# Layer 1's gate and up products as seven block products, with plain f32 products in seven gate tiles and in half of the mixer

## The reference, cut to what matters

```python
def swiglu(h, w_in, w_out):
    gu = h @ w_in                                   # (544, 1024) @ (1024, 5632)
    return (jax.nn.silu(gu[..., :D_FF]) * gu[..., D_FF:]) @ w_out

def pool_mixer(xn, hist, pos, c_w, c_scale):        # layer 1's mixer C
    ...
    y = jnp.einsum('btgc,gce->btge', d, c_w).reshape(b, t, D_MODEL) * c_scale
    return y, ext[:, -C_HIST:]

for layer in range(DEPTH):
    ...
    hp = hp + rms_norm(mp, g[1])
    hp = hp + rms_norm(swiglu(rms_norm(hp, g[2]), ffn_w_in[layer], ffn_w_out[layer]), g[3])
```

## Time and profile before

| | us |
|---|---|
| median of 3 runs | 990.38 (990.16 to 990.46) |
| the profiled execution's own time | 990.5 |
| its span in the trace | 988.6 |
| PE busy | 970.2 (98%) |
| DVE busy | 687.3 (70%) |
| ACT busy | 539.0 (55%) |

### The profile page before, as it was taken

One profiled execution on the slowest core, in us unless ns is written; L12 is line 12 of the kernel. 1 busy time (PEld: TensorE's weight loads), 2 busy tenths in 40 slices (PEclk: granted clock), 3 DMA queues, 4 the chain that ended last, 5 costly groups with the idle time before them and its releaser, 6 DMA issues.

```text
span 988.6 us, 18137 instructions
## 1 busy us (share of the span) xinstructions
PE 970.2 (98%) x7314; PEld 938.8 (95%) x7314; DVE 687.3 (70%) x1024; ACT 539.0 (55%) x979; POOL 49.2 (5%) x57
## 2 busy tenths in 40 slices
PE   7999999899999999999999999999999999999997
PEld 6799899899999999999999999999999999999886
DVE  5487554788799998876599877888755545444643
ACT  5632665666555555466567665775544444444542
POOL 0080220100000000000000000002000000000000
PEclk9999999999999999999999999999999999999999
DMA  8324122556544544357654685666565555556653
GB/s 271 85 69 112 44 65 65 157 166 174 156 128 142 141 134 133 106 164 201 177 167 143 173 213 161 177 174 192 165 175 169 167 160 148 147 165 186 202 171 133
DMA packets 268339, 150.21 MB, mean 152 GB/s; under 512 B 14874, under 2 KB 259458, under 8 KB 268256
## 3 DMA queue, kind: packets, MB, share of 16 engines
q1 hardware_dynamic: 267792, 148.60, 52.0%
q0 software_dynamic: 224, 0.35, 0.1%
q10 hardware_dynamic: 240, 0.10, 0.0%
HBM read 146.45 MB, written 2.58 MB: 151 GB/s over the span
## 4 chain that ended last, share of the span: by engine, by line
PE 92%; DVE 4%; ACT 2%; DMA 1%; issue 1%; ACTq 0%; DVEq 0%
PE ps L746 23%; PE ps L748 22%; PE ps L747 22%; PE ps L1227 6%; PE ps L1229 6%; PE ps L1228 6%; DVE wlo L1959 1%; PE ps L1181 1%; PE ps L1183 1%; PE ps L1182 1%; DMA raw<-in_ffn_w_in_dram 1%; ACT whi L1378 1%; PE ps L996 1%; DMA scale_rows<-in_c_scale_dram 1%; PE ps L940 1%
## 5 line engine op out<-in xcount | busy, mean ns | idle before, releaser
L1959 DVE TENSOR_TENSOR wlo<-raw,whi 128x1024 fp32r<-128x1024 f32 (+3 forms) x278 | 300.4, 1083 | 164.0 <-ACT whi L1378 163.6
L1378 ACT ACTIVATE whi<-raw 128x1024 fp32r<-128x1024 f32 (+3 forms) x278 | 257.5, 930 | 142.2 <-PE ps L748 120.0
L746 PE MATMUL ps<-xhi,whi 128*128 128x256 f32 (+2 forms) x968 | 282.4, 292 | 0.5 <-DVE wlo L1959 0.5
L748 PE MATMUL ps<-xhi,wlo 128*128 128x256 f32 (+2 forms) x968 | 278.2, 287 | 0.0
L747 PE MATMUL ps<-xlo,whi 128*128 128x256 f32 (+2 forms) x896 | 257.6, 287 | 0.0
L746 PEld LDWEIGHTS ps<-xhi,whi 128*128 128x128 f32 x968 | 182.1, 188 | 2.8 <-issue 0.9
L748 PEld LDWEIGHTS ps<-xhi,wlo 128*128 128x128 f32 x968 | 182.0, 188 | 0.0
L747 PEld LDWEIGHTS ps<-xlo,whi 128*128 128x128 f32 x896 | 168.6, 188 | 0.0
L747 PE MATMUL ps<-mlo,whi 128*128 128x256 f32 (+1 forms) x352 | 101.0, 287 | 0.0
L746 PE MATMUL ps<-mhi,whi 128*128 128x288 f32 (+1 forms) x280 | 81.9, 292 | 0.0
L748 PE MATMUL ps<-mhi,wlo 128*128 128x288 f32 (+1 forms) x280 | 81.5, 291 | 0.0
(11 more groups left out here) (294 smaller groups left out, 1981.1 us busy)
## 6 DMA issues: line engine op xcount, KB each, us to landing
raw<-in_ffn_w_in_dram SPq DMA_DIRECT2D x110, 512.0 KB, 4.0
raw<-in_ffn_w_in_dram SPq DMA_DIRECT2D x88, 256.0 KB, 3.4
raw<-in_ffn_w_out_dram SPq DMA_DIRECT2D x48, 384.0 KB, 3.6
raw<-in_ffn_w_out_dram SPq DMA_DIRECT2D x48, 320.0 KB, 3.2
raw<-in_ffn_w_out_dram SPq DMA_DIRECT2D x22, 512.0 KB, 4.4
raw<-in_ab_w_in_dram SPq DMA_DIRECT2D x10, 512.0 KB, 4.8
raw<-in_ab_w_out_dram SPq DMA_DIRECT2D x10, 256.0 KB, 2.9
raw<-in_ab_w_out_dram SPq DMA_DIRECT2D x20, 128.0 KB, 3.3
```

What stands on the lines that cost most here:

```text
L746: pe.matmul(out, wh, xh, start=first, stop=False)
L748: return pe.matmul(out, wl, xh, start=False, stop=last)
L1378: act.activation(whi[:, m % NSPLIT, 0:n], split_source(m), ACT.Copy).then_inc(w_hi, 1)
L1959: dve.tensor_tensor(wlo[:, s, 0:n], split_source(m), whi[:, s, 0:n].bitcast(F32), ALU.subtract)\
```

## The change

Layer 1's gate and up go the way of layer 0's: `fast_first(1)` and `fast_rest(1)` stand where the two passes stood. Half 1's norms and mixer, which had the 44 slots of pass (1,0), have 22 now: STAGE[1,1] is compressed into slots 1 to 16, STAGE[2,1] has its sum at 16 and its residual additions up to slot 21, and everything from `fold` on stands at slots 22 and later, that is, behind the loop over the gate tiles. `splits(1)`, high and low parts of the inner activations, go with `ffn_out(1,1)`.

Units named in PLAIN are not split: PE multiplies the raw f32 tile by the raw f32 x (`xa[1]`), one instruction per chunk in place of three (the trace counts a plain f32 product as two records). Such a tile's place is free only when PE has used it. Mixer C's product for half 1 is plain too, from the raw x (`xf`), its weights from a tile of its own (`c_tile`) and from raw place 3, loaded on ACT's queue.

```diff
-FAST = (0,)
-EARLY = 13
+FAST = (0, 1)
+PLAIN = (5, 7, 9, 12, 15, 17, 19)
...
-    (1, 1): {"sum": 2, "spread": 4, "scale": (4, 5, 7, 8), "fold": 10, "pre": 12, "again": 14, "x": (14, 15, 16, 17),
-             "hist": 9, "rows": (10, 11), "keep": (15, 16),
-             "windows": (20, 23, 24), "ends": (21, 25), "post": (23, 24, 25, 26), "add": (24, 25, 26, 27)},
-    (2, 1): {"sum": 29, "spread": 31, "scale": (31, 32, 34, 35), "fold": 37, "pre": 39, "again": 41,
-             "x": (41, 42, 43, 44)},
+    (1, 1): {"sum": 1, "spread": 3, "scale": (3, 4, 5, 6), "fold": 7, "pre": 7, "again": 9, "x": (9, 9, 10, 11),
+             "hist": 4, "rows": (8, 9), "keep": (9, 10), "c": (11, 12),
+             "windows": (12, 13, 14), "ends": (13, 14), "post": (13, 14, 14, 15), "add": (14, 15, 15, 16)},
+    (2, 1): {"sum": 16, "spread": 18, "scale": (18, 19, 20, 21), "fold": 22, "pre": 22, "again": 23,
+             "x": (23, 24, 25, 26), "s1": (27, 28), "s2": (29, 30), "s34": (31, 32)},
...
+SPLIT_UNITS = [unit[0] != "p" or unit[1] == 0 or unit[2] not in PLAIN for unit in UNITS]
...
-            n = min(range(NRAW if r in FOUR_TILES else NRAW - 1), key=lambda n: (max(last[2 * n:2 * n + 2]), n))
+            n = key[1] % (NRAW - 1) if kind == "p" else \
+                min(range(NRAW if r in FOUR_TILES else NRAW - 1), key=lambda n: (max(last[2 * n:2 * n + 2]), n))
...
-                        sp.wait_ge(w_lo, AT[("tc" if kind == "u2" else kind, *key)] + 1)
+                        m = AT[("tc" if kind == "u2" else kind, *key)]
+                        if SPLIT_UNITS[m]:
+                            sp.wait_ge(w_lo, split_no(m))
+                        else:
+                            sp.wait_ge(w_used, m + 1)
...
+            def plain_pool_products(j):
...
+                        mm = pe.matmul(flat(ring[e % len(ring)], 0, n), tile[:, w], xf[:, 2 * g + k, CUT:CUT + n],
+                                       start=k == 0, stop=k == 1)
...
+                        if plain:
+                            mm = pe.matmul(out, raw_part(load_of(m), UNIT)[:, w], xa[layer][:, k, 0:CUT],
+                                           start=opens and k == ks[0], stop=closes and k == ks[-1], skip_group_check=True)
+                            continue
...
-            ffn_in(1, 0, stepper(pooling(1)))
-            ffn_in(1, 1, idle)
-            ffn_out(1, 1, idle)
+            fast_first(1, stepper(pooling(1)))
+            fast_rest(1)
+            ffn_out(1, 1, stepper(splits(1)))
```

More of the change, by code:

```diff
@@ L122, in unit_sequence @@
     for layer in range(2):
[L123 to L132, removed]
+        seq += [("p", layer, f) for f in range(FC)]
+        for f in range(FC):
+            seq += [("ta", layer, f)] + [("tc", layer, f - 1)] * (f > 0) + [("tb", layer, f)]
+        seq.append(("tc", layer, FC - 1))
         for b in FO_ORDER[layer]:
@@ L166, in split_count @@
 def split_count(layer, b, f):
[L168 to L172, removed]
-    return before + (f + 1 if f < EARLY else EARLY + (f - EARLY) // 2 + 1)
-SPLITS = EARLY + len(LATE) + len(PAIRS)
+    before, early = SPLITS[0] * layer, EARLY[layer]
+    if b != layer:
+        return before + early + len(LATE[layer]) + f // 2 + 1
+    return before + (f + 1 if f < early else early + (f - early) // 2 + 1)
+SPLITS = [early + len(late) + len(PAIRS) for early, late in zip(EARLY, LATE)]
 def z_count(s, d):
@@ L232, in load_of @@
     return LOAD_AT[("u2", *unit[1:]) if unit[0] == "tc" else unit]
[L235 removed]
+FOUR_TILES = [r for r, load in enumerate(LOADS) if load[0] in ("fo", "c")]
 def raw_places():
@@ L470, in late_hi, with overlay @@
-        def late_hi(f, last):
-            i = f - EARLY
-            return xhi[:, i // 2, CUT * (i % 2):CUT * (i % 2 + last - f)]
-        def inner_parts(layer, b, f):
-            if layer not in FAST:
-                hi, lo = (half_a, half_b)[b]
-                return hi[:, f, :], lo[:, f, :]
-            if b:
-                return mhi1[:, f, :], mlo1[:, f, :]
-            return mhi0[:, f, :] if f < EARLY else late_hi(f, f + 1), mlo0[:, f, :]
-        def x_pair(s, b, p):
-            if s in FAST and b == 0:
-                return x32_a[:, 2 * p:2 * p + 2, 0:CUT]
+        def overlay(first, *specs):
+            with ExitStack() as scope:
+                if first:
+                    sb(f"room{first}_{specs[0][0]}", [P, first], F32, scope)
+                return [sb(name, shape, dt, scope) for name, shape, dt in specs]
@@ L1770, in norms @@
                 keep_spread(s, b, 1)
-                if b and s in FAST:
+                if (s, b) == (1, 1):
+                    for i, slot in enumerate(at["keep"]):
+                        yield slot + LATER
+                        keep_rows(i)
+                    return
+                if b and s % 2 == 0:
                     for p, slot in enumerate(at["s1"]):
@@ L1892, in fast_rest @@
                 gate_other(FC - 1)
-                for step in range(len(LATE)):
-                    if step >= 3:
+                for step in range(len(LATE[layer])):
+                    if step in (3, 4):
                         hi_part(u + step)
```

575 lines of the change are left out of this document (277 added, 298 removed).

## The result

The changed kernel takes 1052.5 us (median of 4 runs, 1046.6 to 1053.8) against 990.4: 1.062 times the time before, 95% interval 1.058 to 1.066. The forecast was 1031, its range 1004 to 1043. The direction was right; the loss is 62 us where 40.6 were forecast, and the time lies outside the range.

A forecast was written before the change was run, and what follows sets the result against it. The prediction took PE, busy 98% of the span, to bound the kernel. It summed 990.5 - 138.4 - 140.8 + 146.0 (81.9 work, 64.1 waits) + 172.9 = 1030.2 us, plus 1 for the clock: 1031, range 1004 to 1043.

The forecast's parts named there:

- Products: Layer 1's PE work: first part 81.9 us against 138.4, second part 172.9 against 140.8, a plain product 0.44.
- Held tiles: First part: loads wait until PE has used a plain tile, and ACT's queue delays the next copy; 33.5 us of waits.
- p7's own 1.2: First part: PE waits for tile p7, whose own load ends late; 1.2 us.
- Chain of mixer and norms: First part, slots 9, 15 and 16: PE waits for POOL's power, windows, mixed outputs and last additions; 7.7 us.
- Start: Start of the first part: x's chain, and first loads waiting for low parts in ACT's and DVE's queues; 3.5 us.
- End: Behind the first part's loop: PE waits for fold, norm and DVE's low parts before the second part; 19.4 us.
- The clock: Waits in the first part and at its end: one to five clock falls, near 1 us each; 1 us put in.
- (c): First part: clock falls in each wait and loads take longer; 5 falls, loads of 5 us; 1042 us, chance 0.09.
- (a): First part: the held tiles do not reach PE and the 33.5 us of waits go; 997 us, chance 0.13.
- (b): First part: the end chain and the tiles are hidden, only products count; faster, 970 us, chance 0.06.

## Why the prediction was wrong

By its steps:

- **Products.** Right. PE's work in the first part at full clock is 82.7 (81.9 forecast), the second part 175.15 - 2.5 = 172.7 (172.9), a plain product 0.43 (0.44). The upper bound from the earlier trace rows was 0.475. The Trainium skill's four passes (FP8 and Floating Point Precision, TensorE Precision Notes), priced at 0.119 each, would be 0.476; the trace's 0.43 lies below, 3.6 steps of 0.119. That speaks against this price of a pass and not against four of them: 0.119 is the step of a split product, and no run here shows the passes singly.
- **Held tiles,** 33.5. Right in size, place and mechanism: 4.45, 3.31, 4.93, 1.22, 7.19, 3.28 and 8.90 are 33.3; of the small terms only p7's own 1.2 did not show. Taking the plain tiles away took 29 us of waits away. What the argument lacked is SP's order as the second way in which a held place delays a tile.
- **Chain of mixer and norms,** 7.7: 8.7. **Start,** 3.5: 3.3. **End,** 19.4: 17.65, and the 14.9 of it for DVE's operations one after the other measured 14.95.
- **The clock** is the step that failed: "near 1 us lost in such a start, my estimate of a fall. One to five falls; I put in 1." It measured 23.5 us by the windows, of which 14.7 came back when dummies kept the clock up. Two errors stand in it. The number of falls was guessed from the longest waits, though the forecast itself had a list of waits between 1.2 and 14.9 us, a few microseconds of work apart; 11 falls stood against that list, and even at 1 us each they would have been 11 us and not 1. And the price of a fall was read from four steps of a start that costs some 3 us by the steps ahead of them; behind a wait half clock lasted 3 to 6 us of PE's work, 2.1 us lost. The comparison itself was off as well: the earlier trace rows has 0.111 for a plain record of 128 columns, which does not make 0.22 of 512 split columns by itself; the trace has 0.23.
- **What dummies did not bring back.** The profiled execution with them takes 1037.2, still 7.0 over the forecast's 1030.2 without its clock term. In its trace 3.6 of these are gaps between real products (67.7, forecast 64.1), 3.3 their own time (85.2, forecast 81.9). The gaps are longer in part because PE comes sooner than the other engines; why the products are longer stays open.
- **The rivals.** (c) had the right mechanism, "The clock falls in each wait", and the wrong size: 5 falls at 1 us and 0.8 us of slower loads, 1042. Its slower loads came, but not where PE waits for them: the 19 loads of 512 KB took a median of 5.2 us where they had taken 4.2, two or three going at once when a place comes free late; the first of such a group, on which the wait hangs, landed in 3.9 to 4.2. The Trainium skill, TensorE: Matmul & The Clock Gate, section HAM oscillation, describes this case, bursts between waits that each begin at the low clock; here the trace agrees in the main, with 11 low stretches behind 14 waits. (a) and (b) did not happen: PE's cover of half a tile did not stretch, and even with all tiles split the waits were 33.8, over the 29.9 that the products save there.

## What to carry to other kernels

When an edit opens waits in a stretch where PE had none, count the waits and price the clock with them: here 63 us of waiting cost 23.5 us by the granted clock, of which dummies gave back 14.7, that is 0.23 us for each of waiting (0.37 by the windows). When a price is read from a kernel's start, read the start from its first instruction. Before a tile is given to an engine to hold, look at which queue the next load and the next split of that place stand in: here ACT's queue and SP's handed the delay to copies and loads that have nothing to do with the tile. And work that is freed on engines with slack (DVE and ACT, 70% and 55% busy) was worth less here than what it cost on the engine that bounds: the kernel with no plain gate tile is 46 us faster.

## What the runs showed of the hardware

- A pause of 2.88 us in dense PE work left the clock at full; 4.16 and 8.25 us brought half clock for some 3 and 6 us of the work behind them. Waits of 2.83 and 2.08 us with only 2.0 and 4.4 us of work ahead of them brought it too. Each was seen in one trace.
- Dummy products of 128 columns in the waits held the clock (0.995 to 0.998 over the run) and gave back 14.7 us of 23.5.
- At the kernel's start the clock column shows 1.00, and yet PE's records step at half their later pace until 12.84 us.
- The executions of the changed kernel lie 7.3 us apart (1046.6 to 1053.8) with a mean granted clock of 0.960 to 0.968, the highest in the fastest; those with dummies in eleven waits 1.8. The kernel before lies 0.4 apart beside the changed kernel and 1.3 to 3.8 beside the experiments. That the waits make the scatter is likely and not shown.
- 512 KB loads that start together land one after the other: those at 593.2 us landed after 4.2 and 5.5 us, those at 607.0 after 4.0 and 5.4.
- A DVE subtraction of two SBUF operands that starts beside a POOL subtraction takes until 0.6 us behind POOL's end: 3.18 us in place of 0.75, beside 3.07 of POOL. The Trainium skill, SBUF — State Buffer, section SBUF: two separate sides, says that the two share a port pair which the first takes for its whole instruction; the trace agrees. My expectation for that run had it only as a rival, as DVE slowing down, without its size.
